# Half of the hyena filter spectra made in the combining stage and kept in DRAM, the filter network in the router stage, filter products over 128 rows

## The chip, the cores and the metric

The program runs on one core of a Trainium2 chip. A core has a matrix engine (TensorE, PE in the rows; its weight loads are PEld), a vector engine (VectorE, DVE), an activation engine (ScalarE, ACT), GpSimd (POOL), and SyncE (SP), which here only starts transfers. Each engine has its own stream of instructions and waits on semaphores for the others. The metric is the device time of one launch, in microseconds: the median of several runs.

## The reference

A block with gated linear attention, dilated attention and a mixture of 32 experts is followed by a second block, in which two branches are mixed: a recurrent one (the lru stage) and a hyena one. What the change touches is the hyena branch. Its filters do not depend on the input `x`; they come from a small network over 1024 positions:

```python
h = jnp.sin(freq[0] * (z @ w1 + b1))            # z: 1024 x 33, h: 1024 x 64
h = jnp.sin(freq[1] * (h @ w2 + b2))
h = (h @ w3).reshape(L, HYENA_ORDER, 2, HYENA_WIDTH)   # 2 orders, 2 directions, 1024 channels
filt = h * decay[:, None, None, :]

z = v
for n, gate in enumerate((x1, x2)):             # order 0, order 1
    k = bidir_kernel(filt[:, n, 0], filt[:, n, 1])
    z = gate * fftconv(z, k, filt_bias[n])      # product of spectra, and back
```

Everything is float32. Between the two blocks a combining step adds the two chosen experts' rows to the residual (`x1 + gate0*y0 + gate1*y1`), normalizes it twice (the first block's last norm gives `x2`, the second block's first gives `h`) and turns `h` into `h_T`, channels on partitions.

## The kernel before

The kernel is a chain of stages; all engines meet at a barrier after each. In order: the first mixer, the router (`router_phase`), the experts, `combine_phase`, `lru_phase`, `hyena_inputs_phase`, `gates_phase`, `hyena_phase`, the merge, the second router and its experts, the last norm.

**Router stage.** After the routing numbers are worked out on VectorE (last instruction L1319), GpSimd writes 16 small lists to DRAM by indirect transfers (L1222), waits for them, and loads the list of all blocks (L1226). The other engines have nothing to do then. SyncE starts the loads of the first experts' weights at the start of the stage.

**Combining stage.** Eight tiles of 128 tokens. For tile t VectorE adds the expert rows (`add`, L1992, L1993), makes the first norm (L2003), then the second, and splits the turned tile into an upper and a rest part (`split`, L111, L114). ScalarE makes the sums of squares and roots (L2032, L2035), stores `x2`, and copies the turned tile out of PSUM (L2039). TensorE only turns tiles, eight 128x128 products each. GpSimd gathers the expert rows (L1978), four tiles ahead. Between them the filter network (`FilterNetwork`: `products`, `arguments`, `sines`, L2892 to L2913) makes `hid_T`, 64 rows of 1024, which stays in SBUF until the hyena stage.

**Hyena stage.** Four passes n = 0..3, each an order o and half of the channels h: (0,0), (0,1), (1,0), (1,1). A pass has these steps; the letters are those of the list `program`, which sets TensorE's order, and (n, fh) counts two halves of the frequencies:

- F: the filters of 512 channels. TensorE multiplies `hid_T` (64 rows) by sum and difference of the two directions of `w3` (L3087, 16 products of 512 columns in two PSUM banks); VectorE multiplies each by the decay (L3202, 16 times), corrects the first row (L3180, L3208) and sums the next pass's `w3` (L3190, L3191).
- K: the filters' spectra, 24 products of 512 columns (L3098); ScalarE copies them (L3173), VectorE combines them by butterflies (the K part).
- U: the spectra of the input, 16 products (L3098), copied likewise. VectorE then works on them (the X part: butterflies, the product with K in L3264 and L3266, butterflies back).
- I: the inverse, eight banks of PSUM; VectorE gates each bank (L3224) between instructions of the X part of the next spectra.

A float32 product is recorded as two matmuls. VectorE's order is: the filters of pass n, then K and X parts of (n-1, 1), then those of (n, 0) with the eight gatings of pass n-1 between them. I of pass n-1 waits until the X part of (n-1, 1) is done. SyncE loads everything on one queue, in the order of the code; a load that waits for its buffer holds up all behind it.

## Time and profile before

| | us |
|---|---|
| median of 3 runs | 4470.03 (4469.34 to 4474.12) |
| the profiled execution: its own time | 4476.96 |
| the profiled execution: span | 4475.3 |
| combining stage, first transfer to the first of the lru stage | 1418.7 to 1525.9 |
| hyena stage, first transfer to the first of the merge | 2421.3 to 2992.2 |

Times in rows are microseconds from the start of the span. The engines' busy time in the whole span is 3928.9 us for TensorE, 2916.4 for VectorE, 1790.7 for ScalarE and 307.3 for GpSimd. The two stages above are about 107 and 571 us of the 4475.

### The profile page before, as it was taken

The page shows a single profiled execution, that of the slowest core. Times are in us where ns is not written, and L with a number is a line of the kernel's source. Part 1 is how long each engine was busy: PE and PEld are TensorE (multiplying, and loading weights), DVE is VectorE, ACT ScalarE, POOL GpSimd, SP SyncE. Part 2 cuts the span into 40 slices and gives each one's busy share as a digit, 9 for nine tenths or more (in the row PEclk, how much of TensorE's full clock was granted, in tenths as well). Part 3 has the DMA queues.
Part 4 walks back from the last instruction along what each step waited for, and adds up shares of the span by engine and source line. Part 5 has one row for each costly group of instructions (what it writes and reads, how often), then busy time and mean ns, then how long its engine had stood idle before and what let it go on. Part 6 is the DMA issues. An engine that isn't in the chain of part 4 may idle for free. (4 is left out here: it accounts for less than half of the span.)

```text
span 4475.3 us, 42731 instructions
## 1 busy us (share of the span) xinstructions
PE 3928.9 (88%) x16482; PEld 2929.2 (65%) x16482; DVE 2916.4 (65%) x2694; ACT 1790.7 (40%) x1626; POOL 307.3 (7%) x288
## 2 busy tenths in 40 slices
PE   8989987699996498699898999959769999999996
PEld 3558875588774366487685433547558888888885
DVE  3643444688885667544312677964488888888886
ACT  2234321577774345211000111100137777777773
POOL 0000001201111000000000000000000110101100
PEclk9989998799998699899998899979869999999998
DMA  2001025799996311122322222234539999999996
GB/s 105 1 19 29 14 81 218 266 398 398 399 399 256 106 42 41 52 84 89 122 75 90 88 94 75 77 119 147 194 111 369 377 372 381 372 378 376 371 382 231
DMA packets 418495, 872.69 MB, mean 195 GB/s; under 512 B 22987, under 2 KB 109347, under 8 KB 417992
## 3 DMA queue, kind: packets, MB, share of 16 engines
q1 hardware_dynamic: 386616, 757.75, 47.1%
q0 software_dynamic: 26000, 92.34, 5.9%
q10 hardware_dynamic: 5760, 20.97, 1.2%
q8 instruction: 78, 1.28, 0.1%
q14 instruction: 41, 0.34, 0.0%
HBM read 779.24 MB, written 91.78 MB: 195 GB/s over the span
## 5 line engine op out<-in xcount | busy, mean ns | idle before, releaser
L1773 DVE TENSOR_TENSOR moe_w_rest<-moe_w_w,moe_upper 128x2048 fp32r<-128x2048 f32 x384 | 862.5, 2288 | 194.7 <-ACT moe_upper L1701 117.9
L1701 ACT ACTIVATE moe_upper<-moe_w_w 128x2048 fp32r<-128x2048 f32 x192 | 357.3, 1909 | 304.0 <-PE moe_y_ps L1665 98.2
L1773 DVE TENSOR_TENSOR moe_w_rest<-moe_w_w,moe_upper_w 128x2048 fp32r<-128x2048 f32 x192 | 431.0, 2286 | 19.6 <-ACT moe_upper_w L1716 19.4
L1716 ACT ACTIVATE moe_upper_w<-moe_w_w 128x2048 fp32r<-128x2048 f32 x192 | 357.5, 1910 | 139.8 <-PE moe_up_ps L1649 83.8
L1709 ACT ACTIVATE moe_upper<-moe_w_w 128x2048 fp32r<-128x2048 f32 x192 | 357.3, 1917 | 0.8 <-DMA moe_w_w<-in_w_up_dram 0.8
L1649 PE MATMUL moe_up_ps<-moe_upper,moe_x_upper 128*128 128x512 f32 x768 | 311.3, 405 | 0.0
L1649 PE MATMUL moe_gate_ps<-moe_upper,moe_x_upper 128*128 128x512 f32 x768 | 305.5, 398 | 4.7 <-DVE moe_x_rest L1786 4.7
L1665 PE MATMUL moe_y_ps<-moe_upper_w,moe_hidT_upper 128*128 128x512 f32 x768 | 305.5, 398 | 3.9 <-DVE moe_hidT_rest L1791 3.6
L1649 PE MATMUL moe_gate_ps<-moe_w_rest,moe_x_upper 128*128 128x512 f32 x768 | 304.9, 397 | 0.0
L1649 PE MATMUL moe_gate_ps<-moe_upper,moe_x_rest 128*128 128x512 f32 x768 | 304.5, 396 | 0.0
L1649 PE MATMUL moe_up_ps<-moe_upper,moe_x_rest 128*128 128x512 f32 x768 | 303.8, 396 | 0.0
L1665 PE MATMUL moe_y_ps<-moe_upper_w,moe_hidT_rest 128*128 128x512 f32 x768 | 303.8, 396 | 0.0
L1665 PE MATMUL moe_y_ps<-moe_w_rest,moe_hidT_upper 128*128 128x512 f32 x768 | 303.7, 395 | 0.0
L1649 PE MATMUL moe_up_ps<-moe_w_rest,moe_x_upper 128*128 128x512 f32 x768 | 303.2, 395 | 0.0
L3098 PE MATMUL hyena_fwd_ps<-hyena_filt,hyena_tr 128*128 128x512 f32 x384 | 174.7, 616 | 9.1 <-issue 6.8
L3173 ACT ACTIVATE hyena_K<-hyena_fwd_ps 128x1024 f32<-128x1024 f32 x32 | 32.8, 1024 | 371.2 <-PE hyena_fwd_ps L3098 371.2
L2086 PE MATMUL hyin_proj<-block_h_T_upper,hyin_w_upper 128*128 128x512 f32 x384 | 152.2, 396 | 31.5 <-DVE hyin_w_rest L114 31.5
L1665 PEld LDWEIGHTS moe_y_ps<-moe_upper_w,moe_hidT_upper 128*128 128x128 f32 x768 | 144.2, 188 | 45.1 <-DVE moe_hidT_rest L1791 10.3
L1649 PEld LDWEIGHTS moe_gate_ps<-moe_upper,moe_x_upper 128*128 128x128 f32 x768 | 145.0, 189 | 40.7 <-DVE moe_x_rest L1786 5.5
L1649 PEld LDWEIGHTS moe_gate_ps<-moe_upper,moe_x_rest 128*128 128x128 f32 x768 | 145.0, 189 | 35.2
L1649 PEld LDWEIGHTS moe_gate_ps<-moe_w_rest,moe_x_upper 128*128 128x128 f32 x768 | 145.1, 189 | 35.0
L1665 PEld LDWEIGHTS moe_y_ps<-moe_upper_w,moe_hidT_rest 128*128 128x128 f32 x768 | 144.3, 188 | 34.9
(488 smaller groups left out, 7835.7 us busy)
## 6 DMA issues: line engine op xcount, KB each, us to landing
moe_w_w<-in_expert_w_dram SPq DMA_DIRECT2D x96, 2048.0 KB, 16.6
moe_w_w<-in_w_gate_dram SPq DMA_DIRECT2D x64, 2048.0 KB, 10.5
moe_w_w<-in_w_up_dram SPq DMA_DIRECT2D x64, 2048.0 KB, 9.6
moe_w_w<-in_w_down_dram SPq DMA_DIRECT2D x64, 2048.0 KB, 9.2
tmp_y_rows<-moe_y ACTq DMA_DIRECT2D x32, 512.0 KB, 7.2
hyin_w<-in_w_in_dram SPq DMA_DIRECT2D x24, 512.0 KB, 3.8
tmp_h<-out_xn POOLq DMA_DIRECT2D x16, 512.0 KB, 3.4
tmp_v_x<-hyin_rows POOLq DMA_DIRECT2D x16, 512.0 KB, 3.8
```

The source lines that it names most:

```text
L1649: last = nc.tensor.matmul(out[:, :], lhs[:, k, :], rhs[:, k, :], start=(k == 0 and n == 0), stop=(k == ND - 1 and n == 2))
L1665: last = nc.tensor.matmul(m.y_ps[:, h, :], lhs[:, k, :], rhs[:, k, bass.ts(h, BANK)], start=(start and k == 0 and n == 0), stop=(stop and ...
L1701: act.activation(half(upper1(c), h), half(weights.w1[c % 2], h), ACT.Copy).then_inc(m.w1_rounded, 1)
L1709: act.activation(half(upper3(c), h), half(weights.w3[c % 2], h), ACT.Copy).then_inc(m.w3_rounded, 1)
L1716: act.activation(half(upper2(c), h), half(weights.w2[c % 2], h), ACT.Copy).then_inc(m.w2_rounded, 1)
L1773: dve.tensor_tensor(half(rest, h), half(whole, h), half(upper, h).bitcast(F32), ALU.subtract).then_inc(done, 1)
L2086: last = nc.tensor.matmul(out[:, h, :], lhs[:, k, :], rhs[:, k, bass.ts(h, BANK)], start=(k == 0 and n == 0), stop=(k == ND - 1 and n == 2))
L3098: last = nc.tensor.matmul(fwd_ps[q % 2][:, c, :], tr[:, j, kind, fh, :], rhs, start=(s == 0), stop=(s == len(sums) - 1))
L3173: act.activation(dst, fwd_ps[q % 2][:, :, :], ACT.Copy).then_inc(fwd_copied, 1)
```

## The change

1. The filter network runs at the end of the router stage: its products behind the router's on TensorE, its sine arguments behind the router's last instruction on VectorE, its sines on ScalarE, and the result is stored to DRAM (`hidden`). Its seven small loads stand ahead of the weight loads on SyncE's queue.
2. A class `FilterSpectra` makes, in the combining stage, the filters and the combined spectra of the first half of the channels (h = 0), for both orders. It works in four blocks of 256 channels: (order, quarter) = (0,0), (1,0), (0,1), (1,1). Each block is `make_filters` (16 products of 256 columns), `decay_filters` (8 VectorE instructions, and the first row), and for both halves of the frequencies `transform` (24 products of 256 columns), `copy` (4 on ScalarE), `butterflies` (6 on VectorE), and a store of 1 MB to DRAM (`spectra`), in rows of 1 KB. One block is spread over two tiles of the combining loop. The gathers of expert rows run two tiles ahead instead of four. The turned tile is rounded straight from PSUM by ScalarE, and VectorE subtracts (one VectorE instruction instead of two).
3. In the hyena stage passes 0 and 2 (h = 0) have no F and no K any more; their combined spectra are loaded (2 MB each half) into the K buffers. `MADE` = [1, 3] are the passes that still make theirs.
4. The filter products of passes 1 and 3, and those of `FilterSpectra`, run over 128 rows: `hid_T` and the summed `w3` have 64 rows of zeros below.
5. The order of loads in the hyena stage is another, and semaphores are given back before the merge instead of after it.

```diff
@@ router_phase @@
+                network.load(sp)
...
+                for n in range(2):
+                    network.products(pe, n)
...
+                for n in range(2):
+                    network.sines(act, n)
+                network.store(act)
...
+                for n in range(2):
+                    network.arguments(c, n)
@@ combine_phase @@
-    N_Y = 4
-    NETWORK_AFTER = [0, 3]
+    N_Y = 2
...
+                        held.load_weights(sp)
...
-                        network.load(sp)
+                        held.load_decay(sp, 0)
+                    elif t == 1:
+                        held.load_table(sp)
+                    elif t == NT // 2:
+                        held.load_decay(sp, 1)
...
-                    if t:
-                        split_turned(t - 1)
+                    if t % HF == 0:
+                        held.decay_filters(c, t // HF)
+                    if t >= 2:
+                        rest_of_turned(t - 2)
 
                     dve.wait_ge(n1_ready, t + 1)
                     norm(n1[b], 1, t, n2[b], n2_ready)
-                    if t in NETWORK_AFTER:
-                        network.arguments(c, NETWORK_AFTER.index(t))
-                split_turned(NT - 1)
+                    if t:
+                        held.butterflies(c, t - 1)
+                rest_of_turned(NT - 2)
+                held.butterflies(c, NT - 1)
+                rest_of_turned(NT - 1)
...
-                    if t:
-                        copy_turned(t - 1)
+                    if t >= 2:
+                        held.store(act, t - 2)
+                        round_turned(t - 2)
                     act.wait_ge(n1_ready, t + 1)
                     act.dma_start(x2[bass.ts(t, P), :], n1[b][:, :]).then_inc(stored[b], 16)
                     root(n1[b], 1, t, n1_ready)
-                    if t in NETWORK_AFTER:
-                        network.sines(act, NETWORK_AFTER.index(t))
-                copy_turned(NT - 1)
+                    held.copy(act, t)
+                for t in range(NT - 2, NT):
+                    round_turned(t)
+                    held.store(act, t)
...
-                network.products(pe, 0)
-                for t in range(NT):
-                    b = t % 2
+                def turn(t):
                     pe.wait_ge(n2_ready, t + 1)
                     if t >= 2:
-                        pe.wait_ge(copied, t - 1)
-                    turn_rows(nc, n2[b], turned[b], ident).then_inc(n2_turned, 1)
-                    if t == NETWORK_AFTER[0] + 1:
-                        network.products(pe, 1)
+
+                        pe.wait_ge(h_split, t - 1)
+                    turn_rows(nc, n2[t % 2], turned[t % 2], ident).then_inc(n2_turned, 1)
+
+                for t in range(NT):
+                    if t % HF == 0:
+                        held.make_filters(pe, t // HF)
+                    held.transform(pe, t)
+                    if t:
+                        turn(t - 1)
+                turn(NT - 1)
@@ FilterNetwork @@
+    def store(m, act):
+        act.wait_ge(m.hid_ready, 2)
+        act.dma_start(m.hidden, m.hid[1][:, :]).then_inc(m.stored, 16)
+        act.wait_ge(m.stored, 16)
@@ class FilterSpectra @@
+    HS = HC // 2
+    BLOCKS = [(o, s) for s in range(2) for o in range(HY_ORDER)]
...
+        m.w3_raw = m.sb("w3_raw", [FILT_HID, HY_ORDER, 2, HC])
+        m.w3_sum = m.sb("w3_sum", [P, HY_ORDER, 2, HC])
+        m.bias = m.sb("bias", [1, HY_ORDER, HC])
+        m.decay = m.sb("decay", [P, NT, HS])
+        m.filt = m.sb("filt", [P, 2, HJ, RADIX, HS])
+        m.K = [m.sb(f"K{fh}", [P, RADIX, 2, HS]) for fh in range(HF)]
...
+    def sum_weights(m, dve):
+        dve.memset(m.hid_T[FILT_HID:P, :], 0.0).then_inc(m.rest_cleared, 1)
+        dve.memset(m.w3_sum[FILT_HID:P, :, :, :], 0.0).then_inc(m.rest_cleared, 1)
+        dve.wait_ge(m.w3_loaded, 16 * 2 * HY_ORDER)
+        dve.tensor_tensor(m.w3_sum[0:FILT_HID, :, SUM, :], m.w3_raw[:, :, 0, :], m.w3_raw[:, :, 1, :], ALU.add).then_inc(m.w3_summed, 1)
+        dve.tensor_tensor(m.w3_sum[0:FILT_HID, :, DIFF, :], m.w3_raw[:, :, 0, :], m.w3_raw[:, :, 1, :], ALU.subtract).then_inc(m.w3_summed, 1)
+    def make_filters(m, pe, b):
+        o, s = m.BLOCKS[b]
+        if b == 0:
+            pe.wait_ge(m.rest_cleared, 2)
+            pe.wait_ge(m.w3_summed, 2)
+            pe.wait_ge(m.hid_loaded, 16)
+        for t in range(NT):
+            f = NT * b + t
+            if f >= 2:
+
+                pe.wait_ge(m.filt_ready, f - 1)
+            for d in (SUM, DIFF):
+                last = m.nc.tensor.matmul(m.filt_ps[f % 2][:, d, :], m.hid_T[:, bass.ts(t, P)], m.w3_sum[:, o, d, bass.ts(s, m.HS)], start=True, stop=True)
+            last.then_inc(m.filt_made, 1)
+
+    def decay_filters(m, c, b):
+        o, s = m.BLOCKS[b]
+        dve = c.engine
+        if b:
+
+            dve.wait_ge(m.fwd_made, RADIX * HF * b)
+        dve.wait_ge(m.decay_loaded, 16 * (s + 1))
+        for t in range(NT):
+            f = NT * b + t
+            dve.wait_ge(m.filt_made, f + 1)
+            dve.tensor_tensor(m.filt[:, :, t // RADIX, t % RADIX, :], m.filt_ps[f % 2][:, :, :],
+                              m.decay[:, t:t + 1, :].to_broadcast([P, 2, m.HS]), ALU.mult).then_inc(m.filt_ready, 1)
+        dve.wait_ge(m.filt_ready, NT * (b + 1))
+        end = m.filt[0:1, SUM, 0, 0, :]
+        add_to(c, end, m.filt[0:1, DIFF, 0, 0, :])
+        dve.scalar_tensor_tensor(end, end, 0.5, m.bias[:, o, bass.ts(s, m.HS)], ALU.mult, ALU.add).then_inc(m.end_set, 1)
+
+    def transform(m, pe, u):
+        b, fh = u // HF, u % HF
+        if u == 0:
+            pe.wait_ge(m.tr_loaded, 16 * HJ)
+        pe.wait_ge(m.end_set, b + 1)
+        for i in range(RADIX):
+            q = RADIX * u + i
+            if q >= 2:
+
+                pe.wait_ge(m.fwd_copied, q - 1)
+            for c in (RE, IM):
+                terms = [(kind, part, r, j) for kind, part, r in K_TERMS[i][c] for j in range(HJ)]
+                for n, (kind, part, r, j) in enumerate(terms):
+                    last = m.nc.tensor.matmul(m.fwd_ps[q % 2][:, c, :], m.tr[:, j, kind, fh, :], m.filt[:, part, j, r, :],
+                                              start=(n == 0), stop=(n == len(terms) - 1))
+            last.then_inc(m.fwd_made, 1)
+
+    def copy(m, act, u):
+        fh = u % HF
+        if u >= HF:
+
+            act.wait_ge(m.stored[fh], 16 * (u // HF))
+        for i in range(RADIX):
+            q = RADIX * u + i
+            act.wait_ge(m.fwd_made, q + 1)
+            act.activation(m.K[fh][:, i, :, :], m.fwd_ps[q % 2][:, :, :], ACT.Copy).then_inc(m.fwd_copied, 1)
+
+    def butterflies(m, c, u):
+        c.engine.wait_ge(m.fwd_copied, RADIX * (u + 1))
+        filter_butterflies(c, m.K[u % HF])
+        c.engine.sem_inc(m.ready, 1)
+
+    def store(m, act, u):
+        o, s = m.BLOCKS[u // HF]
+        act.wait_ge(m.ready, u + 1)
+        act.dma_start(m.spectra[o, u % HF][:, :, :, bass.ts(s, m.HS)], m.K[u % HF][:, :, :, :]).then_inc(m.stored[u % HF], 16)
@@ hyena_phase @@
-    program = [("F", 0, 0), ("K", 0, 0), ("U", 0, 0), ("K", 0, 1), ("U", 0, 1)]
+    program = [("U", 0, 0), ("U", 0, 1)]
     for n in range(1, NP):
-        program += [("F", n, 0), ("K", n, 0), ("U", n, 0), ("I", n - 1, 0), ("K", n, 1), ("U", n, 1)]
+        if n in MADE:
+            program += [("F", n, 0), ("K", n, 0), ("U", n, 0), ("I", n - 1, 0), ("K", n, 1), ("U", n, 1)]
+        else:
+            program += [("U", n, 0), ("I", n - 1, 0), ("U", n, 1)]
     program += [("I", NP - 1, 0)]
 
+    place = {step: RADIX * at for at, step in enumerate(step for step in program if step[0] in "KU")}
...
+                def load_k(n, fh):
+                    if n:
+
+                        sp.wait_ge(product_ready, HF * (n - 1) + fh + 1)
+                    sp.dma_start(K[fh][:, :, :, :], spectra[PASSES[n][0], fh]).then_inc(k_loaded[fh], 16)
...
-                load_w3(0)
-                load_decay(0, range(N_DECAY))
-                load_w3(1)
                 for j in range(HJ):
                     sp.dma_start(tr[:, j, :, :, :], forward[:, j, :, :, :]).then_inc(tr_loaded, 16)
-                load_decay(0, range(N_DECAY, NT))
                 for what, n, fh in program:
-                    if what == "F" and n:
-                        load_decay(n, range(N_DECAY, NT))
+                    if what == "F":
+                        load_decay(MADE.index(n), range(N_DECAY, NT))
                     elif what == "U":
-                        if fh == 0 and n + 2 < NP:
-                            load_w3(n + 2)
                         load_u(n, fh)
+                        if n not in MADE:
+                            load_k(n, fh)
                         if (n, fh) == (0, 0):
+                            sp.dma_start(hid_T[0:FILT_HID, :], hidden).then_inc(hid_loaded, 16)
+                            load_w3(0)
+                            load_decay(0, range(N_DECAY))
                             sp.dma_start(inv[:, :, :, :, :], inverse).then_inc(inv_loaded, 16)
-                        if fh == 0 and n + 1 < NP:
-                            load_decay(n + 1, range(N_DECAY))
+                        if (n, fh) == (MADE[0], 0):
+                            load_w3(1)
+                            load_decay(1, range(N_DECAY))
                     elif what == "I":
...
+                pool.memset(hid_T[FILT_HID:P, :], 0.0).then_inc(rest_cleared, 1)
+                pool.memset(w3_sum[FILT_HID:P, :, :], 0.0).then_inc(rest_cleared, 1)
...
-                            nc.tensor.matmul(filt_ps[d][:, :], hid_T[0:FILT_HID, bass.ts(t, P)], w3_sum[:, d, :],
+                            nc.tensor.matmul(filt_ps[d][:, :], hid_T[:, bass.ts(t, P)], w3_sum[:, d, :],
...
-                    if n + 1 < NP:
-                        sum_w3(n + 1)
+                    dve.scalar_tensor_tensor(end, end, 0.5, bias_sb[nth][:, :], ALU.mult, ALU.add).then_inc(end_set, 1)
+                    if nth + 1 < len(MADE):
+                        sum_w3(nth + 1)
...
+                    if n in MADE:
+                        dve.wait_ge(fwd_copied, k_made(n, fh))
+                        filter_butterflies(c, k)
...
+                    if n not in MADE:
+                        dve.wait_ge(k_loaded[fh], 16 * (n // HF + 1))
...
-                filters(0)
                 butterflies(0, 0, None)
                 for n in range(1, NP):
-                    filters(n)
+                    if n in MADE:
+                        filters(MADE.index(n))
```

SyncE, start of the hyena stage, before (`hyena_w_raw` is w3, `hyena_tr` the forward table, `hyena_u` the input's chunks, `hyena_inv` the inverse table):

```order
L3001 DMA hyena_w_raw<-in_filt_w_2_dram 64x2x512
L3005 DMA hyena_bias<-in_filt_bias_dram 1x512
L3014 DMA hyena_decay<-in_filt_decay_dram 128x512 x4
L3001 DMA hyena_w_raw<-in_filt_w_2_dram 64x2x512
L3005 DMA hyena_bias<-in_filt_bias_dram 1x512
L3046 DMA hyena_tr<-in_dft_forward_dram 128x2560 x2
L3014 DMA hyena_decay<-in_filt_decay_dram 128x512 x4
L3001 DMA hyena_w_raw<-in_filt_w_2_dram 64x2x512
L3005 DMA hyena_bias<-in_filt_bias_dram 1x512
L3028 DMA hyena_u<-tmp_v_x 128x2x512 x4
```

The same place now, as far as the third group of the input's chunks (`hyena_K` are the kept spectra):

```order
L3247 DMA hyena_tr<-in_dft_forward_dram 128x2560 x2
L3232 DMA hyena_u<-tmp_v_x 128x2x512 x4
L3218 DMA hyena_K<-tmp_spectra 128x4096
L3256 DMA hyena_hid_T<-tmp_hidden 64x1024
L3202 DMA hyena_w_raw<-in_filt_w_2_dram 64x2x512
L3203 DMA hyena_bias<-in_filt_bias_dram 1x512
L3212 DMA hyena_decay<-in_filt_decay_dram 128x512 x4
L3259 DMA hyena_inv<-in_dft_inverse_dram 128x4096
L3232 DMA hyena_u<-tmp_v_x 128x2x512 x4
L3218 DMA hyena_K<-tmp_spectra 128x4096
L3212 DMA hyena_decay<-in_filt_decay_dram 128x512 x4
L3232 DMA hyena_u<-tmp_v_x 128x2x512 x4
```

The first w3 stood first and now stands behind the table, four chunks and a half of the kept spectra. The second w3 stood ahead of all chunks; where it stands now is the next piece, which goes on where the last one ends:

```order
L3202 DMA hyena_w_raw<-in_filt_w_2_dram 64x2x512
L3203 DMA hyena_bias<-in_filt_bias_dram 1x512
L3212 DMA hyena_decay<-in_filt_decay_dram 128x512 x4
L3242 DMA hyena_z<-tmp_v_x 128x2x512 x4
L3232 DMA hyena_u<-tmp_v_x 128x2x512 x4
```

It is behind the four chunks of U(1, 0), the last of which waits until TensorE has used the first of them.

TensorE in the combining stage, before (`filter_acc` is the network, `combine_turned` a turned tile):

```order
L2892 MATMUL filter_acc<-filter_pos,filter_w 64x512 x2
L1400 MATMUL combine_turned<-ident,combine_n_0 128x128 x8
L1400 MATMUL combine_turned<-ident,combine_n_1 128x128 x8
L2892 MATMUL filter_acc<-filter_hid,filter_w 64x512 x2
L1400 MATMUL combine_turned<-ident,combine_n_0 128x128 x8
L1400 MATMUL combine_turned<-ident,combine_n_1 128x128 x8
```

and now:

```order
L3056 MATMUL held_filt_ps<-held_w_sum,held_hid_T 128x256 x16
L3089 MATMUL held_fwd_ps<-held_filt,held_tr 128x256 x48
L1408 MATMUL combine_turned<-ident,combine_n_0 128x128 x8
L3056 MATMUL held_filt_ps<-held_w_sum,held_hid_T 128x256 x16
L3089 MATMUL held_fwd_ps<-held_filt,held_tr 128x256 x24
L1408 MATMUL combine_turned<-ident,combine_n_1 128x128 x8
L3089 MATMUL held_fwd_ps<-held_filt,held_tr 128x256 x24
L1408 MATMUL combine_turned<-ident,combine_n_0 128x128 x8
```

The network's products are gone from the stage; 64 products for filters and 192 for spectra have come to the 64 of the turned tiles.

## Rows read from the trace of the kernel before

**Rows 1.** The page: TensorE's share, weight loads and the others.

```profile
PE 3928.9 (88%) x16482; PEld 2929.2 (65%) x16482; DVE 2916.4 (65%) x2694; ACT 1790.7 (40%) x1626; POOL 307.3 (7%) x288
```

**Rows 2.** Stretches: start:end, length, busy by engine (instructions), clock (1.00 full), DMA.

```profile
1418.60:1525.90 107.30, 23.01 (x72) 14.01 (x72) 71.33 (x79) 38.35 (x63) 18.54 (x16) 0.50 0.47 168
2421.30:2992.10 570.80, 494.69 (x1152) 233.99 (x1152) 415.60 (x402) 65.54 (x64) 10.16 (x16) 0.88 0.24 84
2426.40:2454.20 27.80, 27.67 (x32) 9.79 (x32) 10.41 (x17) 0.00 (x0) 0.00 (x0) 0.50 0.43 157
2456.40:2478.80 22.40, 22.35 (x49) 9.98 (x50) 1.10 (x2) 3.07 (x3) 0.00 (x0) 0.93 0.26 83
2526.90:2552.10 25.20, 24.73 (x33) 8.55 (x32) 11.83 (x19) 1.02 (x1) 0.00 (x0) 0.59 0.13 42
2597.80:2629.20 31.40, 30.54 (x65) 13.31 (x66) 30.75 (x27) 0.00 (x0) 2.21 (x3) 0.92 0.35 117
2629.20:2649.70 20.50, 20.50 (x49) 9.04 (x48) 15.23 (x14) 3.07 (x3) 0.73 (x1) 1.00 0.14 53
2663.40:2679.30 15.90, 15.83 (x33) 5.29 (x32) 10.37 (x16) 1.02 (x1) 0.00 (x0) 1.00 0.50 160
...
2861.80:2883.20 21.40, 21.28 (x97) 18.45 (x98) 21.02 (x17) 0.00 (x0) 1.65 (x3) 1.00 0.43 146
```

**Rows 3.** Timeline, VectorE, hyena stage: start, length, instruction, [idle before it, until].

```profile
2425.14 0.68 DVE L3190 TENSOR_TENSOR hyena_w_sum<-hyena_w_raw 64x512 f32<-64x512 f32 x1 [9.23 <-DMA hyena_w_raw<-in_filt_w_dram]
...
2493.75 2.29 DVE L3180 TENSOR_TENSOR hyena_U<-hyena_U 128x2048 f32<-128x2048 f32 x1 [6.28 <-ACT hyena_U L3173]
...
2527.91 0.69 DVE L3284 SCALAR_TENSOR_TENSOR hyena_U<-hyena_U 128x512 f32<-128x512 f32 x1
...
2597.66 1.22 DVE L3180 TENSOR_TENSOR hyena_K<-hyena_K 128x1024 f32<-128x1024 f32 x1
...
2605.21 2.29 DVE L3180 TENSOR_TENSOR hyena_U<-hyena_U 128x2048 f32<-128x2048 f32 x1
...
2644.14 0.69 DVE L3284 SCALAR_TENSOR_TENSOR hyena_U<-hyena_U 128x512 f32<-128x512 f32 x1
...
2904.87 0.69 DVE L3180 TENSOR_TENSOR hyena_K<-hyena_K 128x512 f32<-128x512 f32 x1 [3.72 <-ACT hyena_K L3173]
...
2907.58 1.61 DVE L3186 SCALAR_TENSOR_TENSOR hyena_K<-hyena_K 128x512 f32<-128x512 f32 x3
```

**Rows 4.** Transfers: engine, count, KB each, median us from issue to landing.

```profile
hyena_inv<-in_dft_inverse_dram SPq DMA_DIRECT2D x1, 2048.0 KB, 8.5
...
tmp_x<-combine_n ACTq DMA_DIRECT2D x8, 512.0 KB, 4.9
```

**Rows 5.** Timeline, combining stage: VectorE's add, ScalarE's root and copy, the next stage.

```profile
1438.99 1.28 DVE L1992 SCALAR_TENSOR_TENSOR combine_x<-combine_y,gates,combine_x 128x1024 f32<-128x1024 f32 x1 [4.94 <-DMA combine_x<-tmp_x]
...
1443.43 1.06 ACT L2032 ACTIVATE combine_sq<-combine_n 128x1024 f32<-128x1024 f32 x1 [0.33 <-issue]
...
1444.61 0.29 ACT L2035 ACTIVATE combine_rms<-combine_ssum,combine_eps 128x1 f32<-128x1 f32 x1
...
1458.86 1.00 ACT L2039 ACTIVATE block_h_T<-combine_turned 128x1024 f32<-128x1024 f32 x1
...
1525.90 0.39 SPq L2193 DMA_DIRECT2D lru_wx<-in_w_in_dram  x1
```

**Rows 6.** Timeline: the router's end on GpSimd, the network's arguments on VectorE.

```profile
779.51 1.04 POOL L1222 DMA_INDIRECT tmp_row_tok<-router_tok,dest  x1 [35.81 <-issue]
...
805.17 2.35 POOL L1226 DMA_DIRECT2D idx_all<-tmp_row_tok  x1 [5.50 <-DMA tmp_row_tok<-router_tok,dest]
...
1446.40 1.33 DVE L2904 TENSOR_SCALAR filter_arg<-filter_acc,filter_b,filter_freq 64x1024 f32<-64x1024 f32 x1
...
1452.96 0.69 DVE L2909 TENSOR_SCALAR filter_arg<-filter_arg 64x1024 f32<-64x1024 f32 x1
```

**Rows 7.** The gathers of expert rows by tile: least/median/most ns, first and last start.

```profile
L1978 POOL DMA_INDIRECT combine_y<-tmp_y_rows,dest x16: 934/941/1938, 1419.4 to 1468.3; - x16
```

More of the change, by code:

```diff
@@ L1984, in _ @@
                 c.then(dve.memset(eps[:, :], EPS))
+                held.sum_weights(dve)
                 dve.wait_ge(g_loaded, 32)
@@ L2866, in __enter__ @@
         m.turns = m.sb("turns", [H, T])
-        m.hid1 = m.sb("hid1", [H, T])
+        m.hid = [m.sb(f"hid{n}", [H, T]) for n in range(2)]
         m.acc = m.ps("acc", [P, 2, BANK])
@@ L2919, in hyena_phase @@
+def hyena_phase(nc, v_x1, x2_T, hidden, w3, bias, decay, forward, inverse, spectra, z1, z_T):
     PASSES = [(o, h) for o in range(HY_ORDER) for h in range(HY_W // HC)]
     NP = len(PASSES)
-    SUM, DIFF = range(2)
-    RE, IM = range(2)
     N_DECAY, N_CHUNKS, N_U = 4, 3, 3
     SLOTS = range(RADIX)
-    K_TERMS = [([(C0, SUM, 0)], [(S0, DIFF, 0)]),
-               ([(C2, SUM, 2)], [(S2, DIFF, 2)]),
-               ([(C1, SUM, 1), (C3, SUM, 3)], [(S1, DIFF, 1), (S3, DIFF, 3)]),
-               ([(S1_NEG, SUM, 1), (S3, SUM, 3)], [(C1, DIFF, 1), (C3_NEG, DIFF, 3)])]
+    MADE = [n for n, (o, h) in enumerate(PASSES) if h not in HELD_HALVES]
@@ L2964, in hyena_phase @@
         inv_loaded = m.sem("inv_loaded")
+        hid_loaded = m.sem("hid_loaded")
+        k_loaded = [m.sem(f"k_loaded{b}") for b in range(HF)]
         w3_loaded = m.sem("w3_loaded")
@@ L3179, in add @@
                 def add(x, y):
-                    c.then(dve.tensor_tensor(x, x, y, ALU.add))
+                    add_to(c, x, y)
                 def sub(x, y):
@@ L3454, in build_program @@
     part_T, gate_T = dram("part_T", [D, T]), dram("gate_T", [D, T])
+    hidden, spectra = dram("hidden", [FILT_HID, T]), dram("spectra", [HY_ORDER, HF, P, RADIX, 2, HC])
     ident = nc.alloc_sbuf_tensor("ident", [P, P], F32)
```

199 lines of the change are left out of this document (124 added, 75 removed).

## The prediction

> **What bounds the kernel now.** I read the page first. TensorE is busy 88% of the span, VectorE 65% [rows 1], so an edit pays where TensorE stops working or waits. Then the stretches of the two stages that trade work. In the combining stage TensorE is busy 23.0 of 107.3 us and VectorE 71.3 (first row of [rows 2]): the stage is a chain of VectorE and ScalarE steps, and TensorE has room. In the hyena stage it is busy 494.7 of 570.8 us and VectorE 415.6 (its second row): TensorE leads, but VectorE is close behind, and the I step of a pass waits for VectorE's X part. The timeline of VectorE [rows 3] gives the lengths of its parts, and the timeline of the router's end [rows 6] what could hide the network. The sums are made against the profiled execution, 4476.96 us (span 4475.3), which is 6.9 above the median of the runs, 4470.03; I carry differences over to the median.
>
> **Prices.** TensorE, full clock: K takes 20.5 us [rows 2] (the row from 2629.20), so a product of 512 columns 0.855 and U (16 of them) 13.9. Of 256 columns: 96 records, two to a product, in 21.3 us (the last row of [rows 2]), 0.444 each, so 24 take 10.7. F takes 15.9 at full clock, paced by the two PSUM banks, and about 2.3 more until K can start (first row, 2679.3 to 2681.6). VectorE: an X part 34.9 (2493.75 to 2528.6), K part with X part and eight gatings 47.2 (2597.66 to 2644.83), of which K 7.5, and a K part of 256 channels 4.3 (2904.87 to 2909.19) [rows 3].
>
> **The hyena stage: what goes.** TensorE loses F(0) at 27.8, F(2) at 15.9, K(0,0) at 22.4 and three K at 20.5 [rows 2]: 128 us. It doesn't get all of it back. I walk the new order from the first transfer of the stage.
>
> 1. The table (2.6 MB) and the first chunk land at about 10.5: 8.5 for 2 MB [rows 4], and 0.6 MB more. U(0,0) is done at 26.5, 2 us of it for the clock. Its copies, the kept K and w3 (2.4 MB behind the fourth chunk) are there at about 29. X(0,0) runs 30 to 65. U(0,1) waits for 3.6 MB of K, decay and inverse table and lies beside it (39 to 55).
> 2. F(1) runs 65 to 84: 15.9 + 2.3, with 1 for the clock.
> 3. Then VectorE sums the second w3. That load now stands behind the four chunks of U(1,0), and the fourth waits until TensorE has used the first. So VectorE stands still while TensorE does K(1,0) (to 105) and the first chunk of U(1,0) (to 109); the chunk and w3 land some 5.5 later (w3 alone took 3.8 at the start of the stage, 2421.3 to 2425.14 [rows 3]), the sum takes 1.3, and X(0,1) starts at 115.5 instead of 85. It ends at 150.4. Queued behind the waiting sum is all of VectorE; I(0) waits for X(0,1). The price is 30 us at the sum, and 28 at the end, since without it TensorE's U(1,0) would hold I(0) for 2.
> 4. From I(0) to I(1): I 31.4 (the row from 2597.80), K 20.5, U 13.9, the copy 1.2, X(1,1) 34.9: 102. VectorE is now the bound; U(2,0) lies beside.
> 5. From I(1) to I(2): there is no K part to work on, so the gatings wait for TensorE's banks: I 30.6, U(2,1) 13.9, F(3) 18.2, X(2,1) 34.9: 97.6.
> 6. I(2) 31.4, K(3,1) 20.5 and its first copies 1.1: 53.
>
> Sum: 150.4 + 102 + 97.6 + 53 = 403. Before, the K part after K(3,1) started at 2904.87, 483.6 from the stage's start. All behind it is unchanged. **Gain 80 us.** Bounds: 107 if the wait of step 3 is not there; 65 if the starts at steps 1 and 2 cost 15 more (F(1) at half clock alone is 10, below).
>
> **The 128 rows.** F(0) was busy 27.67 of 27.8 us and yet its granted clock was 0.50 throughout; K right behind it had 0.93 and then 1.00; F(1), entered at full clock, fell to 0.59 on average; the third F, as long as its neighbours are full, kept 1.00 [rows 2]. With 64 rows a busy TensorE isn't lifted and can fall; with 128 it is lifted. I take it that zeros count like other rows, so F(1) costs 19 and not 27.8. The Trainium skill (TensorE: Matmul & The Clock Gate, "What's actually happening") says that the clock is held down by default and that activity lifts it, with the time of activity deciding and not the number of instructions; it doesn't mention rows. By that rule alone F(0) would have run at full clock; the trace disagrees with 0.50 over 27.8 busy us.
>
> **The combining stage: what comes.** Away goes the network, two times 7.2 us on VectorE (1446.40 to 1453.65 [rows 6]) and its waits, about 16 of the 107.3. To come are 64 filter products and 192 for spectra, 8 x 4.3 us of butterflies, 32 decay instructions, 32 copies and 8 stores. The walk, from the stage's start:
>
> - The first F needs VectorE after the second `add` and the first norm: `add` could start at 1438.99 because x landed then [rows 5]; x is now behind w3, the gains and a decay of 1 MB, but half the gathers are gone from beside it. I leave it at that: F starts at 24.4, ends at 35.3 (clock low at first), X(0), the first transform, ends at 47.
> - An even transform ends. ScalarE copies it (0.7), makes a root (1.5, 1443.43 to 1444.90 [rows 5]), issues the store of two tiles ago (0.4), rounds a turned tile (1.0), issues the store of x2, makes the second root: 5.6. But the copies of the odd transform go to the K buffer which that store, issued 2.7 ago, must have left. I price the 1 MB in rows of 1 KB at 6.0, between 4.9 (512 KB on the same queue) and 8.5 (2 MB) [rows 4]: the copies start at 8.7, TensorE has stood since 4.7 for want of a PSUM bank, and the odd transform ends at 16.4, or 17.4 with the clock. Turn 1.1, F 8 and 1.6 around it: 28. Even transform 10.7: a round of two tiles is 39 us. VectorE has about 34 of work in it, so it doesn't decide. The first round has no store to wait for: 34.
> - 47 + 34 + 39 + 39 = 159; the last odd transform 17.4; turn, round, butterflies 4.3 and the last store 13.7: 190.
>
> Against 107.3 that is **83 us more**. Bounds: TensorE's own work (24 + 4 x 8 + 8 x 11.8 + a tail of 10, 160) gives +54; everything of it at half clock gives +170.
>
> **The router stage.** The network is 7.2 + 2.3 + 3.7 + 7.2 + 1.1 and a store, about 25 us after VectorE's last instruction, and GpSimd works and waits until its load at 805.17 has landed, 33 us after 779.5 [rows 6]: hidden. What is not: a gather of GpSimd takes 0.94 us, and 1.94 where VectorE reads two SBUF operands at that moment [rows 7]. The network has six such instructions beside the 16 scatters, which are the path. Price between 0 and 10; I take 3. The Trainium skill (GPSIMD Engine Reference, "Key points") says that GpSimd shares its SBUF interfaces with VectorE and contends with instructions in a two-port mode or with two SBUF inputs; the trace agrees with 1.94 against 0.94, and it speaks against this move. Earlier small loads (4 us on SyncE) are hidden behind the routing, which takes 38 us before the lists.
>
> **The sum.** -80 + 83 + 3 = +6: 4476 us at the median, 0.13% more. About 0.2%, 9 us, is what can be told from no change.
>
> **Rivals.**
> - *The stages don't wait as I say (faster).* If w3 arrives before VectorE wants it, or if the store lands in 4 us, the hyena gain is up to 107 and the combining cost some 80. For it: VectorE's wait rests only on the order of loads. Against: the fourth chunk's wait is in the code. 4476 - 27 = 4449. Chance 0.20.
> - *TensorE at half clock in the combining stage (slower).* Today that whole stage is at 0.50 [rows 2], and lru begins so. If pauses of 4 us in each odd transform keep it down, an even transform costs 10.7 more, an odd one 6 more (its pause goes), an F 6: 4 x 22.7 = 91, 4567. It decides as soon as more than a tenth of that stage stays low. For it: such pauses in every round. Against: I steps with waits of 1 to 7 us still had 0.92 [rows 2]. Chance 0.08.
> - *The stores of 1 KB rows are late (slower).* 12 us instead of 6, on three odd transforms and the end: +24, 4500. Nothing in the trace has this shape. Chance 0.12.
> - *Zero rows don't lift the clock.* F(1) costs 27.8, and the kept F twice: +10 and 4 x 3, in part hidden: about 4490. By the skill's rule, which knows no rows, padding would likewise change nothing. Chance 0.15.
> - *My walk, 0.45*, with its own range of 4460 to 4494.
>
> **Chances.** Faster by over 0.2% (under 4461): 0.19 of the first rival, 0.07 of the walk, 0.02 of the last. Within 0.2%: 0.01, 0.25, 0.04. Slower: 0.13 of the walk, 0.08, 0.12, 0.09. That is 0.28, 0.30, 0.42. The range 4447 to 4506 leaves out the half clock and the tail of late stores.
>
> **What will show it.** In the profile after: the stretch from the combining stage's first transfer to the lru stage's first, 190 us, with a clock over 0.8 from the first transform on; ScalarE's copies of odd transforms waiting for a store; in the hyena stage an idle time of about 30 us before VectorE's second sum of w3, ended by a transfer; F(1) at a clock near 1; idle time of TensorE before I(1) of some 20 us; the router stage 0 to 5 us longer. A hyena stage of 463 us instead of 491 would make it wrong on the fast side, a combining stage above 210 on the slow one.

## The result and the profile after

The changed kernel takes 4479.20 us (median of 16 runs, 4475.86 to 4482.60), the kernel before 4470.99 (16 runs, 4465.61 to 4475.81). The ratio is 1.0018, 95% interval 1.0010 to 1.0025: 8 us slower, where 4476 was predicted. The profiled execution took 4477.14 us, its span is 4475.5. One execution among all the runs of this document took 13,101 us at a granted clock of 0.30; it belongs to the run with 64 rows and counts in no median here.

The stages of the profiled execution by windows: the combining stage, its start alone as far as the first transform, the lru stage, the hyena-inputs stage, and the hyena stage. Columns as in [rows 2].

```profile
1420.80:1603.10 182.30, 129.36 (x576) 106.72 (x576) 114.79 (x149) 49.78 (x89) 20.06 (x17) 0.87 0.50 175
1420.80:1456.90 36.10, 12.06 (x32) 8.74 (x32) 17.83 (x22) 5.62 (x10) 8.53 (x8) 0.61 0.93 328
1603.10:1922.40 319.30, 248.88 (x897) 174.50 (x897) 200.80 (x189) 143.38 (x130) 7.10 (x12) 0.88 0.15 43
1922.40:2223.20 300.80, 281.04 (x1281) 233.30 (x1281) 125.61 (x121) 39.76 (x41) 20.39 (x26) 0.96 0.27 84
2503.30:2991.30 488.00, 353.73 (x896) 175.84 (x896) 358.84 (x338) 49.15 (x48) 11.97 (x18) 0.87 0.30 106
```

Combining: 182.3 us for 107.3 [rows 2], 75 more. Hyena: 488.0 for 570.8, 83 less, and VectorE is now as busy there as TensorE (358.8 against 353.7), neither of them for more than 74% of the stage. The clock of the combining stage went from 0.50 to 0.87. The first transfer of the combining stage stands at 1420.8 instead of 1418.7. Against the profile of before these three make -6 us, the lru and hyena-inputs stages +4.6, and everything else +1.3: the two profiled executions differ by 0.2 us, the medians by 8. That gap is taken up by the first experiments.

VectorE in the hyena stage of the changed kernel: the second sum of w3, the first instruction of X(0,1) behind it, and the start of the K part after K(3,1).

```profile
2617.07 0.68 DVE L3397 TENSOR_TENSOR hyena_w_sum<-hyena_w_raw 64x512 f32<-64x512 f32 x1 [31.38 <-DMA hyena_w_raw<-in_filt_w_dram]
...
2618.28 2.28 DVE L2962 TENSOR_TENSOR hyena_U<-hyena_U 128x2048 f32<-128x2048 f32 x1
...
2905.55 0.69 DVE L2962 TENSOR_TENSOR hyena_K<-hyena_K 128x512 f32<-128x512 f32 x1 [3.74 <-ACT hyena_K L3380]
```

Read the bracket of the first row: VectorE stood 31.4 us, and a transfer ended it. SyncE's queue says why that transfer was late. The third row is from the list of SyncE's waits in the same stretch: what it waited for, us in total, times, longest.

```profile
2576.77 35.27 SPq L3232 DMA_DIRECT2D hyena_u<-tmp_v_x  x4
2612.09 0.61 SPq L3202 DMA_DIRECT2D hyena_w_raw<-in_filt_w_dram  x1
...
SPq L3232 <- PE hyena_fwd_ps L3308: 33.4, 1, 33.4
```

The four chunks of U(1,0) took 35.3 us to issue, because the fourth waits until TensorE has used its buffer (33.4 us of them), and w3 is behind them. TensorE's steps in the same stretch, with what it waited for in brackets (one row: start, length, records):

```profile
2568.04 15.50 PE L3297 MATMUL hyena_filt_ps<-hyena_w_sum,hyena_hid_T 128*128 128x512 f32 x28 [10.01 <-DVE hyena_filt L3409]
2585.80 22.41 PE L3308 MATMUL hyena_fwd_ps<-hyena_filt,hyena_tr 128*128 128x512 f32 x48 [2.26 <-issue]
2608.05 13.90 PE L3308 MATMUL hyena_fwd_ps<-hyena_u,hyena_tr 128*128 128x512 f32 x32
2653.27 9.07 PE L3344 MATMUL hyena_inv_ps<-hyena_U,hyena_inv 128*128 128x512 f32 x16 [31.33 <-DVE hyena_U L3489]
...
2754.94 30.05 PE L3344 MATMUL hyena_inv_ps<-hyena_U,hyena_inv 128*128 128x512 f32 x64 [22.34 <-DVE hyena_U L3489]
```

F(1), K(1,0) and U(1,0) run one after another, then TensorE waits 31.3 us for X(0,1), and 22.3 us at I(1). Ahead of I(1) VectorE waits too, for ScalarE's copies of K(1,1) and of U(1,1):

```profile
2706.23 1.23 DVE L2962 TENSOR_TENSOR hyena_K<-hyena_K 128x1024 f32<-128x1024 f32 x1 [5.99 <-ACT hyena_K L3380]
...
2720.03 2.29 DVE L2962 TENSOR_TENSOR hyena_U<-hyena_U 128x2048 f32<-128x2048 f32 x1 [6.28 <-ACT hyena_U L3380]
```

So from I(0) to I(1) neither engine is the bound alone: I(0), K(1,1) and U(1,1) on TensorE, then X(1,1) on VectorE follow one another, and each engine waits for the other.

The combining stage: ScalarE's first two copies of the second, third and fourth odd transform, with the wait ahead of them.

```profile
1511.12 1.08 ACT L3101 ACTIVATE held_K<-held_fwd_ps 128x512 f32<-128x512 f32 x2 [6.51 <-DMA tmp_spectra<-held_K]
...
1549.16 1.08 ACT L3101 ACTIVATE held_K<-held_fwd_ps 128x512 f32<-128x512 f32 x2 [2.14 <-DMA tmp_spectra<-held_K]
...
1582.52 1.09 ACT L3101 ACTIVATE held_K<-held_fwd_ps 128x512 f32<-128x512 f32 x2 [1.49 <-DMA tmp_spectra<-held_K]
```

Each waits for the store that was issued 9.5, 5.1 and 4.8 us before (at 1501.65, 1544.06 and 1577.77). The eight stores from the K buffers, issue to landing:

```profile
DMA to landing us min/median/max: 4.7/4.9/9.6
```

### The profile page after: what moved, and what is told of

Its sections match the earlier page's. It is cut to its first block and busy times, and to the rows that moved or that the text cites. A ratio compares the mean times of both kernels' runs of the same rounds, so it can differ in the third digit from the quotient of the medians.

```text
span 4475.5 us, 43281 instructions
## 1 busy us (share of the span) xinstructions
PE 3906.5 (87%) x16738; PEld 2969.3 (66%) x16738; DVE 2917.3 (65%) x2714; ACT 1789.2 (40%) x1639; POOL 314.1 (7%) x290
## 5 line engine op out<-in xcount | busy, mean ns | idle before, releaser
L1657 PEld LDWEIGHTS moe_gate_ps<-moe_upper,moe_x_rest 128*128 128x128 f32 x768 | 145.1, 189 | 35.3
L1657 PEld LDWEIGHTS moe_up_ps<-moe_upper,moe_x_rest 128*128 128x128 f32 x768 | 144.2, 188 | 34.5
L1673 PEld LDWEIGHTS moe_y_ps<-moe_w_rest,moe_hidT_upper 128*128 128x128 f32 x768 | 144.3, 188 | 34.1
```

The lines of the kernel that those rows point to most:

```text
L1657: last = nc.tensor.matmul(out[:, :], lhs[:, k, :], rhs[:, k, :], start=(k == 0 and n == 0), stop=(k == ND - 1 and n == 2))
L1673: last = nc.tensor.matmul(m.y_ps[:, h, :], lhs[:, k, :], rhs[:, k, bass.ts(h, BANK)], start=(start and k == 0 and n == 0), stop=(stop and ...
```

## Experiments

All medians stand beside 9 to 21 runs of the kernel before on the same chip; ratios are to that kernel, whose own median was 4469.86 to 4471.71 in these series. A changed version ran 5 to 11 times, and once where only a second profile was wanted. Differences of medians between two series are good to about 2 us.

**The kernel before, a second profile** (no edit).

> The kernel before, unchanged, for a second profile of it. In the first its own time was 4476.96 us, 6 us above its median. Theory: whether TensorE falls to half clock in F(1) differs between executions; F(0) is at 0.50 every time, F(1) here is near full clock (some 16 us instead of 25.2), which explains why 128 rows took 19.7 us off the hyena stage against that profile and 9.1 us off the median. Rival: F(1) is at half clock again, and the difference is in stages that nothing touched.

Its own time was 4474.31 us, span 4472.7. By windows: combining and hyena stage, F(0), F(1).

```profile
1421.20:1528.80 107.60, 23.02 (x72) 14.03 (x72) 71.32 (x79) 38.35 (x63) 18.54 (x17) 0.50 0.48 167
2428.40:2987.10 558.70, 479.04 (x1152) 226.94 (x1152) 415.64 (x402) 65.54 (x64) 10.14 (x16) 0.91 0.25 86
2433.50:2461.30 27.80, 27.67 (x32) 9.79 (x32) 10.41 (x17) 0.00 (x0) 0.00 (x0) 0.50 0.42 155
2533.90:2550.20 16.30, 15.80 (x33) 5.28 (x32) 11.89 (x19) 1.02 (x1) 0.00 (x0) 1.00 0.21 64
```

F(0) is as before, to the hundredth. F(1) took 16.3 us at full clock here, 25.2 at 0.59 in the first profile [rows 2]; the hyena stage took 558.7 us, not 570.8. In this execution the lru stage lasted 319.0 us and the hyena-inputs stage 300.7, as in the changed kernel (319.3, 300.8); in the first profile it was 316.2 and 299.3. So the +4.6 us of those stages are not the change's, and of the 83 us that the hyena stage lost against the first profile, 12 were lost by a second execution of the unchanged kernel, 9 of them in F(1). Against it the changed kernel gains 70.7 in the hyena stage and pays 74.7 in the combining stage. Both profiles are single executions, so how often F(1) falls is not known.

**The kernel before with 128 rows.**

```diff
-w3_sum = m.sb("w3_sum", [FILT_HID, 2, HC])
+w3_sum = m.sb("w3_sum", [P, 2, HC])
...
+pool.memset(hid_T[FILT_HID:P, :], 0.0)
+pool.memset(w3_sum[FILT_HID:P, :, :], 0.0)
...
-nc.tensor.matmul(filt_ps[d][:, :], hid_T[0:FILT_HID, bass.ts(t, P)], w3_sum[:, d, :],
+nc.tensor.matmul(filt_ps[d][:, :], hid_T[:, bass.ts(t, P)], w3_sum[:, d, :],
```

> The kernel before with the filter products of all four passes over 128 rows (64 of zeros), nothing else. Theory: F(0), 27.8 us at a clock of 0.50, comes to about 19, K(0,0) behind it from 22.4 to 20.5, F(1) from 25.2 to about 17 and K(1,0) behind it from 25.2 to 21; F(2) and F(3) were at full clock and stay: 22 us less than before (15 to 26), 4449. Rival: rows do not count, no change within 3 us.

4462.30 us, ratio 0.9981 (0.9972 to 0.9990): 9.1 us less, not 22. Windows of the hyena stage, F(0) and F(1):

```profile
2423.90:2975.00 551.10, 467.60 (x1152) 224.54 (x1152) 415.49 (x402) 65.49 (x64) 11.93 (x18) 0.93 0.26 87
2429.10:2447.40 18.30, 18.19 (x32) 6.32 (x32) 10.07 (x15) 0.00 (x0) 0.00 (x0) 0.85 0.63 233
2518.60:2535.00 16.40, 15.75 (x33) 5.23 (x31) 11.97 (x18) 1.02 (x1) 0.00 (x0) 1.00 0.22 64
```

F(0) is 9.5 us shorter. The expectation failed in F(1) and K(1,0): the former was already at full clock in the second profile of before, and the latter took 22.4 us here and 22.3 there. Against that profile the stage is 7.6 us shorter, against the first one 19.7; the medians differ by 9.1, which speaks for the second profile as the usual one.

**The changed kernel with 64 rows.**

```diff
-m.hid_T[:, bass.ts(t, P)], m.w3_sum[:, o, d, bass.ts(s, m.HS)]
+m.hid_T[0:FILT_HID, bass.ts(t, P)], m.w3_sum[0:FILT_HID, o, d, bass.ts(s, m.HS)]
...
-hid_T[:, bass.ts(t, P)], w3_sum[:, d, :],
+hid_T[0:FILT_HID, bass.ts(t, P)], w3_sum[0:FILT_HID, d, :],
```

> The changed kernel with the filter products over 64 rows again, in the combining stage and in passes 1 and 3. Theory: a TensorE that multiplies 64 rows is not lifted and can fall, so F(1) runs at half clock and K(1,0) begins so (10 to 14 us), and the four groups of filter products in the combining stage lose up to 3 us each: 10 to 25 us more than the changed kernel, 4490 to 4504. F(3), which ran at full clock in the kernel before, does not change. Rival: rows do not count, within 3 us of the changed kernel.

4496.84 us in the median of five executions, ratio 1.0054 (1.0040 to 1.0068): 18 us more than the changed kernel. The rows below are from one more execution of the same kernel.

> The same kernel as the run with 64 rows, for a profile of an undisturbed execution. Theory: F(1) and K(1,0) behind it take 10 to 14 us more than in the changed kernel, and the four groups of filter products of the combining stage take 3 us more each, with transforms behind them that begin at half clock: together the 18 us between the medians. Rival: all of it lies in one of the two stages.

4497.02 us. The combining and the hyena stage, F(1) behind its first four records, and the first filters of the combining stage behind their first eight:

```profile
1420.50:1608.40 187.90, 138.15 (x576) 112.46 (x576) 114.79 (x149) 49.76 (x89) 19.99 (x17) 0.83 0.48 169
2509.30:3010.50 501.20, 367.49 (x896) 181.85 (x896) 358.74 (x338) 49.10 (x48) 11.94 (x18) 0.84 0.29 103
2573.80:2598.20 24.40, 24.26 (x28) 8.59 (x28) 9.63 (x16) 0.00 (x0) 0.00 (x0) 0.50 0.31 107
1446.40:1457.10 10.70, 10.61 (x24) 7.85 (x24) 4.05 (x7) 1.24 (x3) 1.12 (x2) 0.50 0.79 321
```

5.6 us more in the one stage and 13.2 in the other. F(1) enters after a wait of 9.7 us and stays at 0.50 to its end, 24.4 us; with 128 rows the same 28 records took 15.5 (above). The combining stage was overestimated: only its first filters ran at 0.50, the later three groups took 7.8 us, as with 128 rows; the rest of what was lost there lies in the transforms behind (12.2 and 13.5 us for 10.6).

**The second w3 early.**

```diff
                         load_u(n, fh)
+                        if (n, fh) == (0, 1):
+                            load_w3(1)
                         if n not in MADE:
                             load_k(n, fh)
...
-                            load_w3(1)
```

> The changed kernel with one load moved: the second w3 stands behind the chunks of U(0,1) on SyncE's queue, not behind those of U(1,0). Theory: VectorE's wait of 31.4 us before the second sum of w3 (at 2617.07 in the changed kernel) goes, X(0,1) starts at about 2585, and I(0) is then held by U(1,0), which ends at 2622, instead of starting at 2653. All behind it moves up by the same: 29 to 31 us less than the changed kernel, 4449 us at a median of 4471 before, ratio 0.995. Rival: the wait stands for work that VectorE has to do later anyway, or the load collides with the kept spectra and delays the start: 0 to 10 us less.

4448.52 us, ratio 0.9947 (0.9933 to 0.9960): 30.7 us less than the changed kernel. The hyena stage took 459.1 us instead of 488.0. TensorE from K(1,0) on:

```profile
2589.49 20.84 PE L3309 MATMUL hyena_fwd_ps<-hyena_filt,hyena_tr 128*128 128x512 f32 x48 [2.26 <-issue]
2610.17 13.90 PE L3309 MATMUL hyena_fwd_ps<-hyena_u,hyena_tr 128*128 128x512 f32 x32
2625.51 7.11 PE L3345 MATMUL hyena_inv_ps<-hyena_U,hyena_inv 128*128 128x512 f32 x16 [1.45 <-DVE hyena_U L3490]
...
2728.88 29.46 PE L3345 MATMUL hyena_inv_ps<-hyena_U,hyena_inv 128*128 128x512 f32 x64 [22.34 <-DVE hyena_U L3490]
```

The wait ahead of I(0) is 1.5 us for 31.3. The one ahead of I(1) is 22.34 in both: TensorE stands there while VectorE does X(1,1), which no load mends. One load's place in a queue was worth 0.69% of the kernel.

**A third K buffer in the combining stage.** To make room the raw w3 lies in the third buffer, which is not written before it is summed.

```diff
+N_K = 3
...
-        m.K = [m.sb(f"K{fh}", [P, RADIX, 2, HS]) for fh in range(HF)]
+        m.K = [m.sb(f"K{b}", [P, RADIX, 2, HS]) for b in range(N_K)]
+        m.w3_raw = m.K[N_K - 1][0:FILT_HID, :, :, :].rearrange("p (o d) a c -> p o d (a c)", d=2)
...
-        if u >= HF:
-            act.wait_ge(m.stored[fh], 16 * (u // HF))
+        if u >= N_K:
+            act.wait_ge(m.stored[u % N_K], 16 * (u // N_K))
```

> The changed kernel with three K buffers in the combining stage instead of two, so that the copies of a transform wait for the store of three transforms ago. Theory: ScalarE's waits of 6.5, 2.1 and 1.5 us for a store go, with TensorE's of 7.5, 3.1 and 1.1 before the odd transforms; two of ScalarE's own steps remain between the banks, so some 3 us per round cannot come back: 8 us less than the changed kernel (5 to 11), 4471 at the median of before. Rival: the odd round is held by ScalarE's roots and roundings and not by the store: under 2 us less.

4466.16 us, ratio 0.9986 (0.9977 to 0.9995): 13.0 less than the changed kernel, a little more than the range named. The combining stage took 171.5 us for 182.3, which is 10.8; TensorE's waits of 7.5, 3.1 and 1.1 us became 0.9, 0.9 and none. The other 2 are within what single profiles differ by: the run with w3 early, which leaves this stage as it was, had it at 184.2 us.

**Both together.**

> The changed kernel with the second w3 loaded early and three K buffers in the combining stage. They act in two stages with a barrier between, so the gains add up: 4479.2 - 30.7 - 13.0 = 4435.5 us (4431 to 4440), ratio 0.992. The difference to the run without kept spectra but with the network moved and 128 rows is what the kept spectra are worth. Rival: that run is as fast, and the kept spectra are worth nothing.

4434.69 us (4431.94 to 4437.40), ratio 0.9914 (0.9901 to 0.9928). Combining 170.4, hyena 459.2.

**The network moved and 128 rows, no spectra kept.**

```diff
@@ router_phase @@
+                for n in range(2):
+                    network.products(pe, n)
...
@@ combine_phase @@
-                network.products(pe, 0)
...
@@ hyena_phase @@
+                sp.dma_start(hid_T[0:FILT_HID, :], hidden).then_inc(hid_loaded, 16)
                 load_w3(0)
```

The arguments, sines and the store go with the products, as in the changed kernel.

> The kernel before with the filter products over 128 rows and the filter network moved to the end of the router stage (its result through DRAM), but no spectra kept. Theory: against the kernel with 128 rows alone (4462.3) the combining stage loses the 14.4 us of VectorE's arguments and about 1 of waits, the router stage gains 2: 4449 us (4445 to 4454). Rival: the arguments stood in the shadow of VectorE's waits for rows, and the move gives nothing or costs the 2 us of the router stage: 4460 to 4464.

4448.62 us, ratio 0.9947 (0.9933 to 0.9960): 13.7 less than with 128 rows alone. The combining stage lasted 88.3 us, 19 less than before; some 3.5 of that are paid back in the router stage (below). So the kept spectra cost 30.6 us as they were written (4479.20 against 4448.62), and are worth 13.9 once the two waits are gone (4434.69). The profiles give the same: 94.0 us more in the combining stage (182.3 against 88.3) and 63.7 less in the hyena stage (488.0 against 551.7). What came with the spectra is in these numbers and was not measured apart: the gathers two tiles ahead, the turned tile rounded from PSUM, the new order of loads and the semaphores given back earlier.

**What holds the start of the combining stage.** Two edits to the last version, each alone. The first, on VectorE and SyncE:

```diff
                         held.load_weights(sp)
+                        held.load_decay(sp, 0)
+                        held.load_table(sp)
                         for j, gain in enumerate((gain1, gain2)):
                             sp.dma_start(g[j][:, :], row(gain).partition_broadcast(P)).then_inc(g_loaded, 16)
-                        held.load_decay(sp, 0)
-                    elif t == 1:
-                        held.load_table(sp)
...
                 held.sum_weights(dve)
+                held.decay_filters(c, 0)
                 dve.wait_ge(g_loaded, 32)
...
-                    if t % HF == 0:
+                    if t and t % HF == 0:
                         held.decay_filters(c, t // HF)
```

> The last version (w3 early, three K buffers) with one more change in the combining stage: the decay of the first filters stands ahead of the first tiles' adds on VectorE, and its decay, then the forward table, ahead of the gains and x of tile 1 on SyncE's queue. In the changed kernel TensorE stood 8.6 us between its eighth and ninth filter record (1438.3 to 1446.9) because the decay products were queued behind add(1), which waited for x. Theory: the first transform starts some 10 us earlier (1447 instead of 1457 by the stamps of the changed kernel), then waits 3 us for ScalarE, whose copies stand behind the roots of tile 0: 7 us less (3 to 11), 4428. Rival: the adds, now behind, hold the tiles' chain, whose steps set the copies: 0 to 3 us less or more, 4432 to 4438.

4435.40 us, ratio 0.9920 (0.9907 to 0.9934): no gain, as the rival said; the stage took 171.9 us for 170.4. TensorE there:

```profile
1439.79 7.83 PE L3058 MATMUL held_filt_ps<-held_w_sum,held_hid_T 128*128 128x256 f32 x24 [0.53 <-DVE held_filt L3071]
1449.39 3.69 PE L3091 MATMUL held_fwd_ps<-held_filt,held_tr 128*128 128x256 f32 x16 [1.77 <-DVE held_filt L3076]
1458.58 13.66 PE L3091 MATMUL held_fwd_ps<-held_filt,held_tr 128*128 128x256 f32 x48 [5.50 <-ACT held_K L3102]
```

The wait among the filters (8.0 us in the last version, 8.6 in the changed kernel) went to 0.5, the first transform began 7 us sooner after the stage's start, and then stood 5.5 us for copies that ScalarE had queued behind the roots of tile 0.

The second, on SyncE's queue alone:

```diff
+                    elif t == 1:
                         held.load_decay(sp, 0)
-                    elif t == 1:
                         held.load_table(sp)
```

> The last version (w3 early, three K buffers) with the load of x of tile 1 ahead of the 1 MB of decay on SyncE's queue. In the changed kernel SyncE was held 7.6 us in issuing that x, behind the decay. Theory: add(1) follows add(0) at once and saves 1.6 us, but the decay lands some 2 us later: 4433 to 4436, no difference that can be measured. Rival: the wait for x was the whole of TensorE's 8.6 us: 5 us or more less.

4431.81 us (4429.81 to 4433.75), ratio 0.9914 (0.9901 to 0.9928). The combining stage took 167.9 us, 2.5 less than in the version it was put on, and the median is 2.9 less; but the kernel before was 1.9 less beside it too (4469.86 against 4471.71), and the two ratios are the same. So the runs don't part the two versions, as the theory said. Its median is the lowest one measured.

## Why the prediction was right, and where it was right by luck

**The hyena stage, walked step by step: right.** From the stage's first transfer the prediction gave X(0,1) at 115.5 us and the K part after K(3,1) at 403; measured were 2618.28 - 2503.3 = 115.0 and 2905.55 - 2503.3 = 402.3. The wait at the sum of w3 was to be 30 us and was 31.4; taking it away was to be worth 28 and was worth 30.7. From I(0) to I(1) 102 were forecast and 101.7 came. From I(1) to I(2) it was 98.1 for 97.6, and from there to the K part 52.5 for 53. One reading in it was wrong: step 4 calls VectorE the bound, though its own sum adds TensorE's three steps to X(1,1), and VectorE stood 6.0 and 6.3 us in that stretch.

**But the 80 us were against an execution that was not typical.** F(1) at 0.59 in [rows 2] was taken as a property of the kernel before, and it is in the 483.6 us from which the 403 were taken. The second profile has it at full clock and the stage 12 us shorter. The gain against that execution is 70.7. The step that failed is "F(1), entered at full clock, fell to 0.59": one record of one execution, read as a rule. The medians say which profile to go by: with the router's 3.5 (below), -70.7 + 74.7 + 3.5 is +7.5 for the measured +8.2, while the first profile gives -82.8 + 75.0 + 3.5, which is -4.3.

**The combining stage: the mechanism right, two sizes off.** +83 was forecast, +74.7 to +75.0 measured. The prediction had every later odd transform wait alike for its store, priced at 6.0 us. The stores took 9.6 us at most and 4.9 in the median, and ScalarE's waits were 6.5, 2.1 and 1.5. Why one store took twice as long is not shown. From the first transform's start the even ones follow at 32.4, 42.4 and 35.4 us where 34, 39 and 39 stood. The first transform ended at 46.8 us, where 47 stood. The tail behind the last even transform was 25.4 us for 31: its odd transform was priced at 17.4 and took 12.6 (1577.8 to 1590.4). So the three rounds missed by -1.6, +3.4 and -3.6, nearly nothing together, and the tail by -5.6, which is most of the error. (A small slip: the lower bound, 160 us of TensorE's own work, is +53 against 107.3 and not +54.) The clock was 0.87 over the stage.

**The two errors cancel.** The hyena gain was 9 us too large against a typical execution and the combining cost 8 too large. The sum, +6, came out beside the measured +8; its terms did not.

**The router stage: the size right, half of the reason missed.** The gap was priced at 3 us within 0 to 10, for scatters slowed by VectorE. The scatters of the changed kernel, durations least/median/most, then the first of them and the load of the list:

```profile
L1223 POOL DMA_INDIRECT tmp_row_tok<-router_tok,dest x16: 967/971/1671, 779.2 to 799.9; - x16
...
779.23 1.04 POOL L1223 DMA_INDIRECT tmp_row_tok<-router_tok,dest  x1 [35.77 <-issue]
...
807.35 2.36 POOL L1227 DMA_DIRECT2D idx_all<-tmp_row_tok  x1 [6.44 <-DMA tmp_row_tok<-router_tok,dest]
```

Two of the 16 took 1.67 us, each at the start of a group of VectorE's instructions with two SBUF operands; the rest took 0.97 to 1.04. That is 1.5 us. From the first scatter to the load of the list it is 28.1 us here and 25.7 before [rows 6]. Over all profiles it was 24.5 to 26.5 in the three with the network in the combining stage, and 28.1 to 30.3 in the eight with the network moved: 3.5 more on average. The other 2 us are a longer wait for the last lists to land, 7.4 to 9.6 us from the last scatter's start for 5.4 to 7.3. The prediction had no term for that, and its cause stays open: the network's own store is issued at that time (800.58), but no run has it elsewhere. The rest of the network lay beside GpSimd's work, as said.

**128 rows.** Rows of zeros lift the clock: F(0) is 9.5 us shorter in the kernel before, and 64 rows cost the changed kernel 18 us. Whether rows with values would lift it sooner, no run shows. By the rule of the Trainium skill as the prediction read it (TensorE: Matmul & The Clock Gate, "What's actually happening"), rows would have changed nothing; the runs decide against that reading: F(0) at 0.50 over 64 rows and at 0.85 over 128. "With 64 rows it can fall" stands too, but it doesn't fall every time: F(3) of the changed kernel with 64 rows kept 13.83 us, while F(1), entered after a wait of 9.7 us, took 24.3.

**The rivals.** "The stages don't wait" (4449, 0.20) was wrong as a forecast. Its price for w3, 27 us, was near: the load moved by hand gave 30.7. For the stores it had 3 us (a combining cost of 80 for 83), and the third buffer gave 13.0. Both together gave 44.5 (4479.20 to 4434.69). "TensorE at half clock" did not come (0.94 from the first transform on). "The stores are late" holds for one store of the three that were waited for, 9.6 us for the priced 6.0. "Zero rows don't lift the clock" fell with the runs above.

## What to carry to other kernels

- Where work is taken out of a stage, read the order of the load queue again: the wait of 31 us came from one 256 KB load left behind a load that waits for its buffer, and cost 30.7 us beside the 70.7 that the hyena stage gained.
- A sum made against one profiled execution inherits its accidents. A second profile of the unchanged kernel moved a gain of 83 us to 71; where a row shows a granted clock below 1 beside equal work at 1.00, profile the kernel again before counting on it.
- Measure a change's parts apart. Here the network's move (-13.7) and the padding (-9.1) paid, and the kept spectra with what came with them, the largest part, cost 30.6 us with their two waits and gave 13.9 without.

## What the runs showed of the hardware

- Matrix products over 64 rows left TensorE at a granted clock of 0.50 (its lower level, 1.2 GHz) for 27.7 busy us in F(0), in both profiles alike; with 64 rows of zeros added the same 32 records took 18.2 us at 0.85.
- Whether such products keep a full clock that they find differs between executions: F(1) took 25.2 us at 0.59 in one and 16.3 at 1.00 in the other.
- 1 MB stored in rows of 1 KB landed in 4.7 to 9.6 us; its median, 4.9, is the one that 512 KB had on the same queue before [rows 4].
- A GpSimd scatter was slowed from 0.97 to 1.67 us only where a group of VectorE's instructions with two SBUF operands began beside it, not through the whole group of 3.7 us; it was the same two of the 16 in all eight profiles with the network moved.
